# Neighbourhood attention loop: the four transposes of a step placed between the two score products

## What is computed

```python
def neighbourhood_attention(q, k, v, k_ctx, v_ctx, rpb):
    ...
        s_loc = jnp.einsum('bqhd,biqjhd->bhqij', q_row, k_win) * scale + jnp.transpose(bias, (0, 2, 1, 3))[None]
        s_ctx = jnp.einsum('bqhd,bkhd->bhqk', q_row, k_ctx) * scale
        s = jnp.concatenate([s_loc.reshape(B, H, GRID_W, kh * kw), s_ctx], axis=-1)
        p = jax.nn.softmax(s.astype(jnp.float32), axis=-1).astype(v.dtype)
        ...
        return (jnp.einsum('bhqij,biqjhd->bqhd', p_loc, v_win)
                + jnp.einsum('bhqk,bkhd->bqhd', p[..., kh * kw:], v_ctx))
```

## Time and profile before

| What | Value |
|---|---|
| time, median of 3 runs | 1665.28 us |
| the runs | 1665.16, 1665.28, 1669.89 us |
| the profiled execution | 1669.46 us |
| its span, first to last instruction | 1667.8 us |
| mean granted TensorE clock | 0.994 |
| PE busy | 1625.8 us (97%) |
| loop of the neighbourhood attention | from about 1123.8 to about 1241 us of the span |

### The profile page before, as it was taken

The page is one execution under the profiler, slowest core; times in us unless marked ns, Lnnn a source line. Parts: engine busy times, 40 slices in busy tenths (PEclk is TensorE's granted clock), DMA queues, the critical chain, the costliest instruction groups (busy, mean ns, idle before and its releaser), DMA issues.

```text
span 1667.8 us, 22101 instructions
## 1 busy us (share of the span) xinstructions
PE 1625.8 (97%) x8707; PEld 1384.7 (83%) x8707; DVE 981.9 (59%) x1266; ACT 774.3 (46%) x1111; POOL 214.9 (13%) x242
## 2 busy tenths in 40 slices
PE   7999999999999999999999999999998999999998
PEld 7888888879898888888878888998886788888887
DVE  5555554576555577777779467537864554435543
ACT  5334433343444456666566388527862333223320
POOL 3680000000000000000004200106740000000000
PEclk9999999999999999999999999999999999999999
DMA  7552123333324344475644221479742232343332
GB/s 254 192 191 74 51 69 109 127 101 127 104 99 141 87 139 123 151 209 174 202 154 144 69 77 61 161 212 246 199 131 80 76 92 84 88 111 91 93 95 78
DMA packets 258375, 211.13 MB, mean 127 GB/s; under 512 B 7827, under 2 KB 241662, under 8 KB 258286
## 3 DMA queue, kind: packets, MB, share of 16 engines
q1 hardware_dynamic: 243646, 162.40, 33.2%
q0 software_dynamic: 11456, 42.72, 7.4%
q10 hardware_dynamic: 3184, 4.77, 0.9%
HBM read 190.25 MB, written 22.76 MB: 128 GB/s over the span
## 4 chain that ended last, share of the span: by engine, by line
PE 85%; DVE 6%; ACT 4%; DMA 2%; POOL 1%; issue 1%; SPq 0%; POOLq 0%; ACTq 0%; DVEq 0%
PE ps L1780 26%; PE ps L1782 26%; PE ps L1781 26%; DVE w_lo L1137 2%; PE ps L1927 1%; ACT w_hi L636 1%; DMA qd<-q_scr 1%; PE ps L2199 1%; ACT mod_tmp L791 1%; POOL sc L2352 1%; PE ps L2191 1%; PE ps L2192 0%; POOL q_lo L2361 0%; DMA cst<-in_consts 0%; PE ps L1913 0%
## 5 line engine op out<-in xcount | busy, mean ns | idle before, releaser
L1780 PE MATMUL ps<-h_hi,w_hi 128*128 128x512 f32 x960 | 376.9, 393 | 6.4 <-DVE w_lo L1137 3.9
L1781 PE MATMUL ps<-h_lo,w_hi 128*128 128x512 f32 x960 | 374.9, 390 | 0.0
L1782 PE MATMUL ps<-h_hi,w_lo 128*128 128x512 f32 x960 | 374.4, 390 | 0.0
L1137 DVE TENSOR_TENSOR w_lo<-w_raw,w_hi 128x2048 fp32r<-128x2048 f32 (+1 forms) x135 | 290.9, 2155 | 117.1 <-ACT w_hi L636 116.6
L636 ACT ACTIVATE w_hi<-w_raw 128x2048 fp32r<-128x2048 f32 (+1 forms) x135 | 240.5, 1782 | 111.2 <-PE ps L1782 107.4
L1780 PEld LDWEIGHTS ps<-h_hi,w_hi 128*128 128x128 f32 x960 | 180.8, 188 | 45.9 <-DVE w_lo L1137 5.5
L1782 PEld LDWEIGHTS ps<-h_hi,w_lo 128*128 128x128 f32 x960 | 180.8, 188 | 38.1
L1781 PEld LDWEIGHTS ps<-h_lo,w_hi 128*128 128x128 f32 x960 | 180.9, 188 | 36.4
L1780 PE MATMUL ps<-xg_hi,w_hi 128*128 128x512 f32 x352 | 137.4, 390 | 0.0
L1782 PE MATMUL ps<-xg_hi,w_lo 128*128 128x512 f32 x352 | 137.2, 390 | 0.0
L1781 PE MATMUL ps<-a_lo,w_hi 128*128 128x512 f32 x352 | 137.0, 389 | 0.0
(11 more groups left out here) (356 smaller groups left out, 3137.1 us busy)
## 6 DMA issues: line engine op xcount, KB each, us to landing
mod_raw<-in_l_w_mod POOLq DMA_DIRECT2D x24, 1024.0 KB, 7.8
w_raw<-in_w_ffn_in SPq DMA_DIRECT2D x44, 512.0 KB, 4.8
w_raw<-in_l_ffn_w_up SPq DMA_DIRECT2D x44, 512.0 KB, 4.4
w_raw<-in_w_in SPq DMA_DIRECT2D x40, 512.0 KB, 4.8
w_raw<-in_l_na_w_qkv SPq DMA_DIRECT2D x24, 512.0 KB, 4.6
w_raw<-in_w_mem_kv SPq DMA_DIRECT2D x16, 512.0 KB, 3.9
masked_scr<-mb POOLq DMA_DIRECT2D x16, 384.0 KB, 3.8
w_raw<-in_w_ffn_out SPq DMA_DIRECT2D x16, 384.0 KB, 3.7
```

The lines of the kernel that those rows point to most:

```text
L1137: v.tensor_tensor(wlo[s][:, 0:size], raw[s][:, 0:size], whi[s][:, 0:size].bitcast(F32), ALU.subtract).then_inc(w_lo, 1)
L1780: mm(o, w_h, x_h, start=first, stop=False, **kw)
L1781: mm(o, w_h, x_l, start=False, stop=False, **kw)
L1782: return mm(o, w_l, x_h, start=False, stop=last, **kw)
```

## The change

In the steps 1 to 59 PE issues the four transposes of `g` in other places: the first ahead of the first score matmul of `g + 4`, the second between the two score matmuls, the third and fourth behind the second. The waits of the transposes (`ns_norm`, `np_l`) are now met ahead of the first transpose, behind the waits of the scores (`ns_exp`, and `qd_in` at `tau == 0`), since `na_scores` waits before it calls `between`. `np_ps` still rises with the last transpose. Step 0 and the steps 60 to 63 are as they were.

```diff
-            def na_scores(g):
+            def na_scores(g, between=None):
...
+                if between:
+                    between(0)
                 mm(o, qd[head % 2][:, 0, P * tau:P * tau + P], keys, start=True, stop=False)
+                if between:
+                    between(1)
                 mm(o, qd[head % 2][:, 1, P * tau:P * tau + P], keys, start=False, stop=True).then_inc(ns_ps, 1)
 
-            def na_transpose(g):
+            def na_transpose(g, chunks=range(4)):
+                if 0 in chunks:
+                    na_transpose_ready(g)
+                for c in chunks:
+                    last = nc.tensor.transpose(bank(prob_bank(g))[:, c * P:c * P + P], sc[:, g % 4, c * P:c * P + P], ident)
+                if 3 in chunks:
+                    last.then_inc(np_ps, 1)
+
+            def na_transpose_ready(g):
+
                 pe.wait_ge(ns_norm, g + 1)
                 if g >= 2:
                     pe.wait_ge(np_l, g - 1)
-                for c in range(4):
-                    last = nc.tensor.transpose(bank(prob_bank(g))[:, c * P:c * P + P], sc[:, g % 4, c * P:c * P + P], ident)
-                last.then_inc(np_ps, 1)
...
             for g in range(NA_G):
-                na_transpose(g)
-                if g == 0:
-                    pe.wait_ge(evac, b + n)
-                    na_scores(3)
-                if g + 4 < NA_G:
-                    na_scores(g + 4)
+                if 0 < g < NA_G - 4:
+                    na_scores(g + 4, between=lambda c: na_transpose(g, (c,)))
+                    na_transpose(g, (2, 3))
+                else:
+                    na_transpose(g)
+                    if g == 0:
+                        pe.wait_ge(evac, b + n)
+                        na_scores(3)
+                        na_scores(4)
                 if g:
                     na_values(g - 1)
```

## The result

The changed kernel takes 1675.25 us (median of 5 runs, 1674.73 to 1675.56), the kernel before beside it 1666.33 us (5 runs, 1665.16 to 1669.89). The ratio is 1.0049, with a 95% interval from 1.0038 to 1.0060: slower by 6 to 10 us.

What follows compares the result with a forecast made beforehand. The two-step loop from transposes through ACT, DVE and POOL back to transposes was taken to bound the kernel. 0.9 up to step 17 and 7.7 after gave 8.6, taken as +8.5: 1673.8 us, range 1670.7 to 1677.5.

Steps and rivals of the forecast that it cites:

- the loop: Transposes of g, ACT high part, DVE low part and reciprocal, POOL normalisation, transposes of g+2; slack 0.07 us.
- The loop goes from 3.26 to 3.73 us: Two steps lengthen by both score products, 0.47 us, now standing before the end of the transposes.
- Eight steps 15.39: Four loops of 3.73, plus 0.20 for POOL's low part and 0.27 for ACT's head copy, against 13.95 us.
- The first sixteen steps +0.9: Late query landings set the pace up to step 17, so only +0.5 to +1.0 us, taken as 0.9.
- The last four steps 0: Steps 60 to 63 are written as before, so they add nothing.
- PE's own step unchanged, 1.64: PE's work per step without waits stays 1.64 us; bounds were a gain of 0.05 and a loss of 0.11.
- The rule on the weight load: Load cost grows with stationary columns, so the last transpose, followed by a smaller load, would save some 0.05 us a step.
- Rival 1: Weight loads are hidden and PE's step shrinks: +7.4 us, or some +4.2 at the large saving; chance 0.13.
- rival 2: Score-product weight loads are laid bare below one transpose: loop 3.84, +10.9 us, 1676.2; chance 0.13.
- rival 3: Faster: the loop has far more slack and PE's step decides, -3.0 or -11.2 us; chance 0.04.
- rival 4: Loss taken up by waits elsewhere; if the steps after the first 16 did half as much, +4, 1669.3; chance 0.04.
- The waits view would have POOL 25 times or more: Sign in the changed profile: PE waits for POOL's normalisation some 25 times or more, 8 to 12 us in all.

Runs made afterwards that it cites:

- the late signal: Kernel before, with ACT's high part in steps 1 to 59 waiting for the second score product instead of the last transpose; ratio 1.0041, 1676.26 us.
- the four transposes left together: Changed order, but with all four transposes unsplit between the two score products; ratio 1.0008 to the kernel before, 1669.89 against 1668.38 us.
- the loop opened: DVE takes the reciprocal of g+2 ahead of the low part of g; 1663.66 us on the kernel before, 1664.66 on the changed one.

## Why the prediction was right

Predicted were 1673.8 us and +8.5; measured 1675.25, +8.9 (6 to 10). By its steps:

- *PE is not what bounds a pair of steps, the loop is*, and it had 0.07 us of slack. Right: it is shown by the late signal, by the four transposes left together, and by the loop opened.
- *The loop goes from 3.26 to 3.73 us.* Measured 3.75: the transposes' part grew by 0.43 to 0.48, and the handing over from POOL to PE by 0.06. The prediction left the handing over at 0.05 and started from 3.26, the chain's length; its own steady step gives 3.21 (1171.34 to 1174.50, and 0.05), which is what its slack of 0.07 is counted from. 3.21 + 0.48 + 0.06 is 3.75, so the small distance of 0.02 comes from two errors, of 0.05 and 0.06, that nearly cancelled: luck in the size, not in the mechanism.
- *Eight steps 15.39.* Measured 15.55. Three of the four pairs were right within 0.03 (3.75, 3.74, 3.90 for 3.73, 3.73, 3.93). The fourth, with ACT's copy of a head, was put at 2.09 + 1.91 = 4.00 and took 2.09 + 2.06 = 4.15. There POOL ends at 1174.37 + 1.04 = 1175.41 and the transpose starts only at 1175.67, 0.26 later (last rows of the timeline). This is a step that opens a head: its first transpose now stands behind four waits (the second piece of the order shown with the change), and the sum had priced the handing over at the 0.05 of a transpose with two. That made 43 steps 8.5 instead of 7.7 us. The prediction's check of its rules on the kernel before (13.97) was a little kind: it took 0.2 for ACT's copy there and 0.27 in the forecast; with 0.27 in both the check gives 14.04 against the 13.95 of the windows.
- *The first sixteen steps +0.9, since the landings hold the pace anyway.* Measured 1.2 to 2.1, 1.65 on the mean. The mechanism was only partly right: the waits for landings did shrink (one of 1.0 us is left), but from step 8 to 16 the changed kernel takes 15.3 to 15.4 us, its own pace, and step 16 starts 0.26 and 0.35 us after its normalisation, so the loop and not the landing sets step 16. This term was sized too small, by nearly half.
- *The last four steps 0.* Measured 0.2.
- *PE's own step unchanged, 1.64.* Measured 1.66 in the short steps, as in the late signal, and with the loop opened some 0.01 more a step. The rule on the weight load, by which the last transpose would save 0.05, does not show: no step of the changed order is shorter than 1.64. Rival 1 is refuted by this, rival 2 by the loop of 3.75 where it had 3.84, rival 3 by the idle time of PE in 27 steps, and rival 4 by the 8.5 us from step 17 on, where it had half.
- *The waits view would have POOL 25 times or more.* 27 waits and 7.9 us on PE are there, but only six waits and 1.5 us of them under POOL's name; a reader who looks for POOL alone would take the theory for wrong.

The sum of the terms in the trace is 1.65 + 8.5 + 0.2 = 10.3 us, against 8.6 summed before. The terms were too small by 1.7 us together, in the handing over where a head opens, in the first sixteen steps and in the last four. That the medians came out at 8.9, so near to 8.5, is luck too: at the same mean clock the difference is 9.8.

## What to carry to other kernels

Where several engines pass a group round and the next group but one starts only when that is done, count the whole circle and divide by the groups under way, and compare this with the busiest engine's step: an order that is free for the busiest engine costs its full length if it lies in a circle without slack, as here (0.07 us of slack, 0.47 added). Signals that others wait for should leave before work that nobody waits for, so here the transposes stay together; the score products, whose results are needed only by later steps, can stand behind them, or one of them ahead, at next to no cost. And it is worth a look what closes the circle. Here it was the order of two instructions on one engine: a reciprocal of 0.15 us behind a low part that it does not need.

## What the runs showed of the hardware

**A stretch at half clock that comes in some executions.** The first profile of the kernel before has PE's granted clock at 0.50, its lower level of 1.2 GHz, from about 935 to 941 us. The engine was never idle there; before the clock fell, at 934.5, it ran sixteen one-column products and the first of the eight of line 2147. Timeline row and window of the first profile of before:

```profile
934.12 1.52 PE L2147 MATMUL ps<-cst,sqacc 128*128 128x1 f32 x8
```

```profile
936.00:938.00 2.00, 2.00 (x12) 2.00 (x11) 0.15 (x1) 0.00 (x0) 0.00 (x0) 0.50 0.78 273
```

and the same stretch in the second profile of the same kernel:

```profile
936.00:938.00 2.00, 2.00 (x19) 2.00 (x18) 0.00 (x0) 0.00 (x0) 0.00 (x0) 1.00 0.56 193
```

The same work ran at full clock there, and that execution had a span of 1664.2 us instead of 1667.8, although its loop was 0.7 us longer. Of the fourteen profiles of this document eight have a stretch at 0.50 in this place. Some also have one at about 17 us, and with both taken together they explain much of when the first transpose of step 1 starts, in work that is the same in all the kernels:

| Time at 0.50 before the loop, about | profiles | first transpose of step 1, us |
|---|---|---|
| none | 3 | 1122.9, 1123.2, 1123.8 |
| 3 us | 2 | 1122.4 (changed, first), 1125.8 |
| 7 us | 7 | 1125.2 to 1127.4 (before, first) |
| 10 us | 2 | 1127.7, 1128.9 (changed, second) |

Within a row the starts still differ by up to 3.4 us, so something else has a part in it, and what that is stays open. In all, 6.5 us of an execution's time are decided ahead of the loop, two thirds of what the change costs. This is why the runs blur what the traces repeat within 0.01 us from step 17 on, and why comparing runs at the same mean clock helps. It is a reading of traces side by side; no run was made to move the clock.

**Handing over grows with the waits before an instruction.** From POOL's end to PE's first transpose, in steps where PE waits for POOL, it was 0.05 us with two waits, 0.11 with three and 0.26 with four, of which one is for a DMA. With two waits fewer it was 0.05 with one wait and 0.14 with two, one of them for the DMA, and eight steps took 0.15 us less.
